# A hybrid decoder layer: log-forget sums on VectorE, full-height spread matmuls, a later page stage and the first up products ahead of the last norm tile

## What is computed

```python
xn = rmsnorm(x, g_mix); z = xn @ w_in
logf = log_sigmoid(fz + b_fgate)                  # 8 heads
c = cumsum(logf, axis=1)                          # over the tokens
s = q @ k.T * dh**-0.5 + c_q - c_k                # forgetting attention, causal
...                                               # dilated windows, 3 groups x 4 heads
w = softmax(stack(lses)); o = sum(w * outs)       # the three groups combined
merged = sigmoid(gate_fox) * y_fox + sigmoid(gate_dil) * y_dil
x = x + merged @ w_mix_out
x = x + cross_attn(rmsnorm(x, g_xattn), mem_kv)
u = rmsnorm(x, g_ffn) @ w_up                      # 2 x 2816 columns
h = b_conv + sum(w_conv[i] * up[:, i:i + S] for i in range(3))
x = x + (gelu(gate) * val) @ w_down
```

## Time and profile before

| | |
|---|---|
| median of 3 runs | 2814.0 us |
| profiled execution, own time | 2817.78 us |
| its span, first to last instruction | 2815.8 us |
| mean granted TensorE clock | 0.990 |
| TensorE busy | 2760.6 us, 98% |
| VectorE busy | 1105.0 us, 39% |
| ScalarE busy | 528.5 us, 19% |
| GpSimd busy | 142.2 us, 5% |

### The profile page before, as it was taken

How to read it: one execution, slowest core, us unless ns; L and a number is a source line. 1 busy time by engine, 2 the same in 40 slices (tenths; PEclk the granted TensorE clock), 3 DMA queues, 4 the chain that set the end, 5 groups by cost and what they waited for, 6 DMA issues and landing times.

```text
span 2815.8 us, 37732 instructions
## 1 busy us (share of the span) xinstructions
PE 2760.6 (98%) x14324; PEld 1865.8 (66%) x14324; DVE 1105.0 (39%) x2734; ACT 528.5 (19%) x1159; POOL 142.2 (5%) x267
## 2 busy tenths in 40 slices
PE   8999999999999999999999999998999999999998
PEld 7655555777665555556644567545888888888887
DVE  2145553232243223333222022335666666654332
ACT  2233322221201112111011022230221122110002
POOL 0000001020101112100000000000000000000000
PEclk9999999999999999999999999998999999999999
DMA  5000101100115778876520400332543543143201
GB/s 188 22 12 9 58 1 55 57 19 19 44 29 153 208 209 254 243 207 191 191 85 30 179 30 30 123 131 54 182 142 123 168 141 123 30 164 106 83 28 64
DMA packets 207161, 294.63 MB, mean 105 GB/s; under 512 B 20781, under 2 KB 145086, under 8 KB 205942
## 3 DMA queue, kind: packets, MB, share of 16 engines
q1 hardware_dynamic: 148150, 187.76, 20.5%
q10 hardware_dynamic: 42976, 89.39, 9.8%
q0 software_dynamic: 15856, 15.07, 2.2%
HBM read 268.20 MB, written 63.35 MB: 118 GB/s over the span
## 4 chain that ended last, share of the span: by engine, by line
PE 94%; DMA 2%; DVE 1%; issue 1%; SPq 1%; ACT 0%; ACTq 0%; DVEq 0%
PE psum L2379 20%; PE psum L939 10%; PE psum L2759 10%; PE psum L1844 8%; PE psum L1928 7%; PE psum L515 5%; PE psum L2081 4%; PE psum L686 3%; PE psum L1267 3%; PE psum L702 3%; PE psum L1852 3%; PE psum L1303 2%; PE psum L1283 2%; PE psum L2055 2%; PE psum L713 2%; DMA arena<-in_cache_fox_kv 1%
## 5 line engine op out<-in xcount | busy, mean ns | idle before, releaser
L2379 PE MATMUL psum<-arena 128*128 128x272 f32 x2464 | 567.5, 394 | 0.0
L2379 PEld LDWEIGHTS psum<-arena 128*128 128x128 f32 x2464 | 469.8, 191 | 97.3
L939 PE MATMUL psum<-arena 128*128 128x512 f32 (+3 forms) x960 | 316.9, 481 | 1.4 <-ACT arena L568 1.4
L1844 PE MATMUL psum<-arena 128*128 128x368 f32 (+1 forms) x768 | 305.4, 498 | 1.7 <-ACT arena L1880 1.1
L2759 PE MATMUL psum<-arena 128*128 128x256 f32 (+1 forms) x1584 | 288.1, 356 | 0.0
L2759 PEld LDWEIGHTS psum<-arena 128*128 128x128 f32 (+1 forms) x1584 | 252.4, 178 | 34.7 <-issue 3.2
L1928 PE MATMUL psum<-arena 128*128 128x512 f32 x512 | 237.0, 596 | 0.8 <-issue 0.8
L939 PEld LDWEIGHTS psum<-arena 128*128 128x128 f32 (+1 forms) x960 | 194.9, 250 | 62.4 <-issue 35.1
L762 DVE CUSTOM_DVE_ANT_0 arena<-psum,arena 128x256 f32<-128x256 f32 (+2 forms) x224 | 95.2, 457 | 213.2 <-PE psum L686 213.1
L2482 DVE TENSOR_TENSOR arena<-arena,psum 128x272 f32<-128x272 f32 (+2 forms) x330 | 113.6, 378 | 158.8 <-PE psum L2379 158.0
L1844 PEld LDWEIGHTS psum<-arena 128*128 128x128 f32 x768 | 125.6, 194 | 68.4 <-issue 47.0
(11 more groups left out here) (226 smaller groups left out, 2780.6 us busy)
## 6 DMA issues: line engine op xcount, KB each, us to landing
arena<-in_cache_fox_kv SPq DMA_DIRECT2D x128, 256.0 KB, 4.3
arena<-in_cache_fox_kv ACTq DMA_DIRECT2D x128, 256.0 KB, 4.2
out_win_s<-in_cache_win_kv ACTq DMA_DIRECT2D x8, 4080.0 KB, 15.1
arena<-in_w_up SPq DMA_DIRECT2D x44, 512.0 KB, 6.3
arena<-in_w_down SPq DMA_DIRECT2D x14, 1408.0 KB, 6.3
arena<-in_cache_win_kv SPq DMA_DIRECT2D x16, 1024.0 KB, 7.9
arena<-in_cache_mem_kv SPq DMA_DIRECT2D x16, 1024.0 KB, 6.8
arena<-in_w_in SPq DMA_DIRECT2D x9, 1024.0 KB, 7.9
```

The lines of the kernel that those rows point to most:

```text
L939: last = pe.matmul(banks[c0 // 512][p0:p0 + r, 0:n], xn_tile(k, g, t), wD[g][:, k, w0:w0 + n], start=(k == 0), stop=(k == KD - 1))
L1844: last = pe.matmul(banks[0][:, 0:cw], w[:, k, :], xnT[:, k, c0:c0 + cw], start=(k == 0), stop=(k == KD - 1))
L2379: last = pe.matmul(banks[n % 8][:, 0:Q4], w[:, k, :], r[:, k, Q4 * p:Q4 * p + Q4], start=(k == 0), stop=(k == 3))
```

## The change

- `lf_dve` adds up the log forgets of preceding tiles (six additions of 128x8), and `forget_sums_pe` takes one matmul with ones per tile: 15 matmuls in place of 36.
- The bias spreads take all 128 rows of `cT`, whose other rows GpSimd clears at the start.
- The combine's spreads are two matmuls of 64 columns of weights with all 128 rows each, from columns of the identity; `head_rows` leaves the table of constants. VectorE clears all rows of the statistics ahead of them.
- The page stage is due from 869 to 1223, the first five value pages right behind the combine.
- The third norm is due until 2066 in place of 2072. The first four up products (`a11 b11`, `a12 b21`) are issued in the weave, ahead of the last tile's transposes; the old rows are transposed behind them, into banks 1 and 2.
- The order of the up products is changed (`a12 b21` second), with it VectorE's order, the banks, and the counts that the down loads wait for.

```diff
-    combine=(776, 860), ga=(715, 1010), gb=(1010, 1448), foxprep=(765, 775), fox=(862, 1222), dilprep=(1226, 1228),
+    combine=(776, 860), ga=(715, 1010), gb=(1010, 1448), foxprep=(765, 775), fox=(869, 1223), dilprep=(1226, 1228),
...
-    memkv=(1592, 1650), q=(1650, 1814), x=(1692, 1856), c=(1848, 2040), n3=(1880, 2072), xp=(1872, 2012))
+    memkv=(1592, 1650), q=(1650, 1814), x=(1692, 1856), c=(1848, 2040), n3=(1880, 2066), xp=(1872, 2012))
...
+            pool.memset(cT, 0.0).then_inc(s_clear, 1)
...
+            for t in range(2, NQ):
+                yield at("p0")(0.06) + 0.1 * t
+                dve.wait_ge(fp["lf_out"], t - 1)
+                dve.tensor_tensor(earlier(t), earlier(t - 1), lfn[:, t - 1, :], ALU.add).then_inc(fp["lf_out"], 1)
...
-            pe.wait_ge(fp["lf_out"], 1)
+            pe.wait_ge(fp["lf_out"], NQ - 1)
             for t in range(NQ):
...
-                for q in range(t):
-                    pe.matmul(out, lfn[:, q, :], ones, start=(q == 0), stop=False)
+                if t:
+                    pe.matmul(out, earlier(t), ones, start=True, stop=False)
...
-                    pe.matmul(banks[q % 2], ident[0:HF, 2 * j + n // 2:2 * j + n // 2 + 1].to_broadcast([HF, P]),
-                              cT[0:HF, n % 2 * 512:(n % 2 + 1) * 512], start=True, stop=True).then_inc(fp["computed"], 1)
+                    pe.matmul(banks[q % 2], ident[:, 2 * j + n // 2:2 * j + n // 2 + 1].to_broadcast([P, P]),
+                              cT[:, n % 2 * 512:(n % 2 + 1) * 512], start=True, stop=True).then_inc(fp["computed"], 1)
...
-                    pe.matmul(banks[3 + m % 4], cst["head_rows"][32 * c:32 * c + HD, j * P:(j + 1) * P],
-                              stT[32 * c:32 * c + HD, g, 0, :], start=True, stop=True).then_inc(cb["spread"], 1)
+                    for a in range(2):
+                        row = 32 * c + 2 * j + a
+                        last = pe.matmul(banks[3 + m % 4][64 * a:64 * a + 64, :], ident[:, row:row + 1].to_broadcast([P, 64]),
+                                         stT[:, g, 0, :], start=True, stop=True)
+                    last.then_inc(cb["spread"], 1)
...
-                    dve.memset(stT[0:RH, 2, 0, :], 0.0)
+                    dve.memset(stT[:, :, 0, :], 0.0).then_inc(s_clear, 1)
...
-                    yield fox_turn_due(6) - 0.1
+                    yield at("combine")(1) + 0.5
...
-                    yield fox_turn_due(6 + n)
+                    yield at("combine")(1) + 1 + n
...
+        def first_products_pe(pe):
+            for x in range(2):
+                for p in range(2):
+                    yield at("c")(1.02) + 0.1 * (2 * x + p)
+                    if x == 0 and p == 0:
+                        pages_over(pe, pg_x)
+                        pe.wait_ge(*nth(n3, "kept", 2 * 5))
+                    up_product(pe, 0, x, p)
...
         def mlp_pe(pe):
+            old_rows_pe(pe)
             for j in range(NF):
...
+            w, r = ((a11, b11), (a12, b21), (s2_sum, t2_sum), (s1_sum, t1_sum), (s3, t3_sum),
+                    (s4_sum, b22), (a22, t4_sum))[x]
...
-                dve.wait_ge(mp["product"], NPR * (j - 1) + 6)
+                dve.wait_ge(mp["product"], NPR * (j - 1) + 8)
...
-            sp.wait_ge(mp["product"], UP_DONE - NPR + 6)
+            sp.wait_ge(mp["product"], UP_DONE - NPR + 8)
             down_load(sp, "x0", (0, 0), 0)
```

More of the change, by code:

```diff
@@ L81, in make_constants @@
     c["new_sum"] = a.reshape(P, -1)
[L82 to L86, removed]
     inv = np.float32(10000.0) ** (-np.arange(32, dtype=np.float32) / np.float32(32))
@@ L222, in build @@
         ident, ones = cst["ident"], cst["ones"]
+        spare = take(256)
         G_NAMES = ("g_mix", "g_xattn", "g_mem", "g_ffn")
@@ L2344, in mlp_sp, with old_rows_pe @@
                     sp.dma_start(wu[i], w_up[:, :, c:c + P]).then_inc(wu_in[i][0], 16)
-        def mlp_pe(pe):
+        def old_rows_pe(pe):
             landed(pe, old_in, 1)
-            pages_over(pe, pg_x)
+            pe.wait_ge(*nth(xo, "added", 2 * TT))
             for q in range(2):
+                if q:
+                    pe.wait_ge(*nth(n3, "kept", 2 * TT))
                 for f in range(22):
-                    last = pe.transpose(banks[6 + q][:, f * 16:(f + 1) * 16],
+                    last = pe.transpose(banks[1 + q][:, f * 16:(f + 1) * 16],
@@ L2352, in mlp_pe @@
                                         old_rows[0:16, (22 * q + f) * P:(22 * q + f + 1) * P], ident[0:16, 0:16])
             last.then_inc(mp["old_turned"], 1)
-            pe.wait_ge(*nth(n3, "kept", 2 * TT))
-            pe.wait_ge(*nth(xo, "added", 2 * TT))
-            for j in range(NF):
[L2357 to L2361, removed]
-                    for p in range(2):
[L2363 to L2378, removed]
-                            last = pe.matmul(banks[n % 8][:, 0:Q4], w[:, k, :], r[:, k, Q4 * p:Q4 * p + Q4],
-                                             start=(k == 0), stop=(k == 3))
-                        last.then_inc(mp["product"], 1)
@@ new lines, in first_products_pe, with mlp_pe @@
+        def first_products_pe(pe):
[6 more added lines that the diff above has]
+                    up_product(pe, 0, x, p)
+        def mlp_pe(pe):
+            old_rows_pe(pe)
+            for j in range(NF):
+                for x in range(2 if j == 0 else 0, 7):
+                    for p in range(2):
+                        up_product(pe, j, x, p)
@@ new lines, in up_product @@
+        def up_product(pe, j, x, p):
+            gate, val = wu[2 * (j % 2)], wu[2 * (j % 2) + 1]
+            a11, a12, a22 = gate[:, 0:4, :], gate[:, 4:8, :], val[:, 4:8, :]
+            s3 = val[:, 0:4, :]
+            w, r = ((a11, b11), (a12, b21), (s2_sum, t2_sum), (s1_sum, t1_sum), (s3, t3_sum),
+                    (s4_sum, b22), (a22, t4_sum))[x]
+            n = NPR * j + 2 * x + p
+            if x == 0 and p == 0:
+                landed(pe, wu_in[2 * (j % 2)], j // 2 + 1)
+            if x == 2 and p == 0:
+                pe.wait_ge(mp["w_sums"], 4 * j + 3)
+                if j == 0:
+                    pe.wait_ge(*nth(n3, "kept", 2 * TT))
+                    pe.wait_ge(mp["t_sums"], 3 * 5)
+            if n == 6:
+                pe.wait_ge(mp["old_kept"], 1)
+            if x == 5 and p == 0:
+                pe.wait_ge(mp["w_sums"], 4 * j + 4)
+            if j == 0 and x == 6 and p == 0:
+                pe.wait_ge(mp["t_sums"], 3 * 5 + 1)
+            if n >= 8:
+                product_drained(pe, n - 8)
+            for k in range(4):
+                last = pe.matmul(bank_of(j, x, p), w[:, k, :], r[:, k, Q4 * p:Q4 * p + Q4],
+                                 start=(k == 0), stop=(k == 3))
+            last.then_inc(mp["product"], 1)
@@ L2386, in bank_of @@
         def bank_of(j, x, p):
-            return banks[(NPR * j + 2 * x + p) % 8][:, 0:Q4]
+            return banks[(NPR * j + 2 * x + p + 3) % 8][:, 0:Q4]
         def unit_parts(x, half, p):
@@ L2525, in mlp_dve @@
                 for p in range(2):
-                    dve.wait_ge(mp["product"], NPR * j + 3 + p)
+                    dve.wait_ge(mp["product"], NPR * j + 5 + p)
                     dve.wait_ge(mp["kept"], 2 * j + p + 1)
@@ L2529, in mlp_dve @@
                         dve.wait_ge(mp["quarters"], NPR * j)
-                    dve.tensor_tensor(u2_sum[p], first_half(0, p), bank_of(j, 1, p), ALU.add).then_inc(mp["quarters"], 1)
+                    dve.tensor_tensor(u2_sum[p], first_half(0, p), bank_of(j, 2, p), ALU.add).then_inc(mp["quarters"], 1)
                 for p in range(2):
-                    dve.wait_ge(mp["product"], NPR * j + 5 + p)
                     dve.wait_ge(mp["quarters"], quarter_done(j, "u2", p))
-                    onto(0, 1, p, u2_sum[p], bank_of(j, 2, p))
+                    onto(0, 0, p, None, bank_of(j, 1, p))
                 for p in range(2):
                     dve.wait_ge(mp["product"], NPR * j + 7 + p)
+                    onto(0, 1, p, u2_sum[p], bank_of(j, 3, p))
+                for p in range(2):
+                    dve.wait_ge(mp["product"], NPR * j + 9 + p)
                     if j and p == 0:
@@ L2539, in mlp_dve @@
                         dve.wait_ge(mp["tailed"], 3 * 2 * j)
-                    onto(1, 0, p, u2_sum[p], bank_of(j, 3, p))
+                    onto(1, 0, p, u2_sum[p], bank_of(j, 4, p))
                 for p in range(2):
                     dve.wait_ge(mp["quarters"], quarter_done(j, "u3", p))
-                    onto(1, 1, p, first_half(1, p), bank_of(j, 2, p))
+                    onto(1, 1, p, first_half(1, p), bank_of(j, 3, p))
                 if j + 1 < NF:
                     weight_sums(dve, j + 1)
-                for p in range(2):
-                    dve.wait_ge(mp["product"], NPR * j + 9 + p)
-                    onto(0, 0, p, None, bank_of(j, 4, p))
                 for p in range(2):
@@ L2583, in convout_pe @@
             for f in range(11):
```

(9 more changed lines are left out.)

24 lines of the change are left out of this document (14 added, 10 removed).

## The result

| | before | changed |
|---|---|---|
| median, us | 2814.58 (4 runs, 2808.69 to 2819.57) | 2787.15 (4 runs, 2782.3 to 2787.32) |
| profiled execution, own time | 2817.78 | 2787.32 |
| its span | 2815.8 | 2785.5 |
| mean granted clock | 0.990 | 0.996 |

The ratio is 0.988 with a 95% interval of 0.9855 to 0.9905, so the changed kernel is faster, by 1.2%. The medians lie 27.4 us apart, the two profiled executions 30.5 us. The forecast was 2783 with a range of 2773 to 2799.

The account below looks back on a forecast made before the run. TensorE was taken to bound the kernel, busy 98% of the span. Gains of 0.4 + 4.5 + 7.8 + 6.7 + 2.5 + 9.7 = 31.6 us gave a forecast of 2783 us, range 2773 to 2799.

Parts of the forecast that it names:

- Bound: Whole kernel: TensorE, busy 98% of the span and 94% of the chain, sets the time.
- Start: Kernel start: a table load smaller by 131 KB lets TensorE's first instruction begin sooner, 0.4 us gained.
- Forget sums: Forget-sum matmuls: 21 fewer at 0.216 us each, 4.5 us less on TensorE; VectorE's added sums cost zero.
- Low clock in the pair stages: Bias spreads: 128 rows in place of 8 remove the low clock; 7.8 us gained, bounds 0 and 8.5.
- Combine: Combine spreads: low clock goes, 6.7 us gained; paired 64-column matmuls run side by side at no cost, upper bound 11.
- Page stage: Page stage due later, first value pages earlier: shorter page waits; 2.5 us gained, bounds 5 gained and 4 lost.
- First products: MLP's first up products issued before the last transposes: 11.4 us sooner less a 1.7 us clock fall; 9.7 gained.
- Order of the up products: The 22 up-product passes: new order, banks and down loads cost zero, hidden by the bank ring.
- rival C: Up-product passes: late weight sums make every pass pay, slower; 2827 us with 2 us each, chance 0.03.
- Sum: All terms together: 31.6 us gained, giving 2786.2 from the profiled execution or 2782.4 from the median; forecast 2783.

Follow-up runs that it names:

- e11: Kernel before, with only the 128-row bias spreads and GpSimd's clearing of `cT` added; 2807.22 us, ratio 0.9947.
- e7: Changed kernel with 36 forget-sum matmuls again in place of 15, VectorE's six additions kept but unused; 2790.67 us, ratio 0.9903.
- e1: Changed kernel with the 16 bias spreads back at 8 rows of operand, same columns and count; 2800.08 us, ratio 0.9922.
- e9: Changed kernel with 64 rows of operand in the bias spreads in place of 128; 2791.4 us, ratio 0.9889.
- e3: Changed kernel with the page stage due from 862 to 1222 again, value loads still early; 2795.99 us, ratio 0.9925.
- e4: Changed kernel with the first five value-page loads at their old place, at the seventh key page; 2791.26 us, ratio 0.9905.
- e5: Changed kernel with the first four up products behind the last tile's transposes and the old rows, new product order kept; 2793.93 us, ratio 0.9913.
- c0: The changed kernel itself, measured once more without edits; 2793.39 us, ratio 0.9902 against the kernel before.
- e8: Changed kernel with the 44 old-row transposes made plain matmuls over all 128 buffer rows, 16 moving columns; 2798.6 us, ratio 0.9936.
- e2: Changed kernel with the 24 combine spreads taking 4 rows of operand in place of 128; 2794.34 us, ratio 0.9905.
- e6: Changed kernel with the fifth up product put between the last tile's transposes and the old rows; 2783.95 us, ratio 0.9855.

## Why the prediction was right, step by step

- *Bound.* TensorE at 98% and 94% of the chain: what was taken from it showed in the span, and the rows of the table add up to it.
- *Start.* 0.4 forecast, nothing found. The first TensorE instruction began at 8.01 us in place of 7.89 and the forget sums at 98.8 in place of 98.2; in the other traces with the smaller table they began at 99.6 to 100.5, and in e11, which has the full table, at 99.1. What starts the first tile is, by the profile, the load of the forget bias, last on its queue; VectorE's first reciprocal behind it came at 9.84 us in place of 9.50. I had read the first TensorE wait and not the next one, and the smaller table brought neither forward.
- *Forget sums.* 4.5 forecast, 4.6 by e7.
- *Low clock in the pair stages.* 7.8 forecast, with an upper bound of 8.5; 9.8 in the trace (14.4 - 4.6), 9.8 by e11, 11.4 by e1. The mechanism was right. I took 0.7 off for holes, and there was only 0.2 us more idle time. The other 1.3 us, above my bound, are not the clock: I had let the spreads' own time stand, and it fell (e9 shows 0.7 of it).
- *Combine.* 6.7 forecast. 5.2 lies between the spreads and 1.7 behind them, from a fall at 857 us that the page row of the table holds: 6.9. The pairs cost nothing, as line 1936 had shown.
- *Page stage.* 2.5 forecast, 4.3 - 1.7 = 2.6 in the trace, and this agreement is luck. The fall at 1161 us, which I had not foreseen, took 1.7 us in the trace after; without a fall in either kernel the stage gained 4.3. The reason was only half right. The later due number gives it (e3), but not by less waiting for key pages, and the early value pages show no part (e4). Which of the smaller waits makes up the 4 us is open.
- *First products.* 9.7 forecast, 8.4 in the trace, 7.1 of it by e5. The fifth product began 21.15 us behind the start of line 1936's products, where I had 20.8. The clock stayed low for 6.8 us, and the part of it in the product stream, 5.5 us at 0.55, cost 2.5 where I had charged 1.7. So the size of the fall was the term that was off, and it differs between traces: in e1, e4 and e7 the fall lasted half as long, and the same stretch took 580.0 to 580.3 us in place of 581.0.
- *Order of the up products.* Nothing forecast, nothing found; rival C did not come.
- *Sum.* 31.6 forecast, 30.5 between the profiled executions. That it came so near is in part luck: 2.0 us too little for the pair stages stand against 1.0 too much at the start, 1.3 at the first products, and 1.5 that the stretches which the change does not touch took longer. The medians gave 27.4, and 26.0 in c0's batch, so whole runs show 4 to 6 us less than the forecast. Why is not shown; the stretch described last, which the change does not touch and I had not seen, moves a run by more than that.
- The Trainium skill ("TensorE: Matmul & The Clock Gate", Part 1) has the gate follow how busy the engine is. In e1's pair stages the clock fell at 100% busy behind 8-row matmuls and in e11's it did not; by that rule alone both would be the same. Its Part 4 says that transposes do not count as busy the same way, and the fall behind the old rows agrees; e8 shows that plain matmuls with little to stream let it fall too.

## What to carry to other kernels

Read the granted clock per stage before you look for idle time: a TensorE that is 100% busy can still be at half speed (19.8 us in c0, below). Here a matmul with few rows of operand cost no more with all rows, the others cleared (3.78 us for four with 8 rows, 3.77 with 128), and the pair stages were 9.8 us shorter (e11). Where a chain over ScalarE and VectorE holds up the last tile, long products that need only earlier tiles are the work to put there.

## What I had not expected

From the end of the page stage to the mixer's output nine traces took 184.1 to 186.5 us and five 191.7 to 197.5, though no edit touches this stretch; the changed kernel itself is in both groups, with 186.5 and, as c0, 193.6. The sample tokens' gate products (line 1872) stand there: 48 matmuls with 128 rows and 64 moving columns. Timeline and windows of the changed kernel's first trace, then of c0's:

```profile
1370.03 10.90 PE L1872 MATMUL psum<-arena 128*128 128x64 f32 x96 [1.93 <-DMA arena<-in_w_br_dil]
```

```profile
1370.00:1380.00 10.00, 9.97 (x90) 10.00 (x90) 0.69 (x1) 0.00 (x0) 0.00 (x0) 1.00 1.05 388
```

```profile
1366.99 19.82 PE L1872 MATMUL psum<-arena 128*128 128x64 f32 x96 [1.95 <-DMA arena<-in_w_br_dil]
```

```profile
1370.00:1380.00 10.00, 10.00 (x49) 10.00 (x48) 0.00 (x0) 0.00 (x0) 0.00 (x0) 0.50 0.96 361
```

The same 96 instructions take 10.9 or 19.8 us. In c0 the clock fell right behind the wait for the gate weights, and did not come back in the 20 us of short matmuls; in the other trace the same wait had no fall behind it. The five traces with the long form are c0, e2, e5, e6 and e11. That it makes up most of the spread of the runs is likely and not shown, for a run without a trace has only its mean clock: of c0's four runs the fastest, 2785.52 us, had 0.997 and the others 0.993 to 0.995. Longer products in that place would be the next thing to try; it was not tried.
